# The down weight pieces of the experts are split into high and low parts whole instead of by halves

## The reference

```python
logits = h @ router                                   # (256, 8)
top_v, top_i = lax.top_k(logits, 2)
wts = jax.nn.softmax(top_v, axis=-1)
comb = jnp.sum(one_hot(top_i, 8) * wts[..., None], axis=-2)
return sum(comb[..., e:e + 1] * swiglu(h, w1[e], w3[e], w2[e]) for e in range(8))
# swiglu(h, w1, w3, w2) = (silu(h @ w1) * (h @ w3)) @ w2
# w1, w3: (1024, 3584) of each expert; w2, the down weights: (3584, 1024)
```

## Time and profile before

| what | value |
|---|---|
| runs | median 2206.45 us of 3 (2204.03 to 2206.86) |
| profiled execution | 2205.63 us |
| its span, first to last instruction | 2203.8 us |
| mean granted TensorE clock | 0.982 of full speed |
| PE matmul busy | 2104.9 us (96%) |
| DVE busy | 1772.6 us (80%) |
| ACT busy | 1176.0 us (53%) |
| experts, about 1187 to 2197 us: PE busy from 1240 to 2040 | 800.0 of 800 us |
| the same, DVE | 709.4 of 800 us |
| the same, ACT | 585.6 of 800 us |
| the same, DMA engines busy | 0.92 to 0.94, 347 to 368 GB/s |

### The profile page before, as it was taken

How to read it: one execution, slowest core, us unless ns; L and a number is a source line. 1 busy time by engine, 2 the same in 40 slices (tenths; PEclk the granted TensorE clock), 3 DMA queues, 4 the chain that set the end, 5 groups by cost and what they waited for, 6 DMA issues and landing times.

```text
span 2203.8 us, 28714 instructions
## 1 busy us (share of the span) xinstructions
PE 2104.9 (96%) x10154; PEld 1737.3 (79%) x10154; DVE 1772.6 (80%) x2268; ACT 1176.0 (53%) x1388; POOL 42.5 (2%) x84
## 2 busy tenths in 40 slices
PE   8988999997999998879997999999999999999997
PEld 6765888876888886758996888888888888888886
DVE  7777877877677676877866988888898988989895
ACT  3316333324333332534555777777677777777674
POOL 0000000000000000000000000000000000000000
PEclk9999999998999999999997999999999999999999
DMA  8500233453444443403464999989898999989893
GB/s 320 192 33 1 96 110 134 172 200 115 171 152 153 171 153 114 163 25 120 163 236 157 388 356 349 373 323 368 335 371 334 366 349 342 370 336 371 331 364 123
DMA packets 77289, 512.44 MB, mean 233 GB/s; under 512 B 8738, under 2 KB 9890, under 8 KB 22820
## 3 DMA queue, kind: packets, MB, share of 16 engines
q1 hardware_dynamic: 65700, 469.59, 56.7%
q0 software_dynamic: 11520, 41.95, 5.3%
HBM read 510.46 MB, written 1.05 MB: 232 GB/s over the span
## 4 chain that ended last, share of the span: by engine, by line
PE 82%; DVE 11%; ACT 3%; issue 2%; DMA 2%; SPq 0%; DVEq 0%; ACTq 0%; POOL 0%; POOLq 0%
PE bank L844 9%; PE bank L842 9%; PE bank L843 9%; PE bank L863 5%; PE bank L865 5%; PE bank L864 5%; PE bank L596 4%; PE bank L598 4%; PE bank L597 4%; PE bank L761 2%; PE bank L762 2%; PE bank L763 2%; PE bank L737 2%; PE bank L747 2%; PE bank L748 2%
## 5 line engine op out<-in xcount | busy, mean ns | idle before, releaser
L971 ACT ACTIVATE down_high<-W 128x1024 fp32r<-128x1024 f32 x224 | 237.1, 1064 | 139.3 <-PE bank L865 139.1
L1341 DVE TENSOR_TENSOR up_b_low<-W,up_b_high 128x2048 fp32r<-128x2048 f32 x112 | 256.6, 2291 | 56.5 <-ACT up_b_high L964 56.5
L1348 DVE TENSOR_TENSOR down_low<-W,down_high 128x1024 fp32r<-128x1024 f32 x224 | 271.8, 1223 | 31.6 <-ACT down_high L971 21.7
L1335 DVE TENSOR_TENSOR up_a_low<-W,up_a_high 128x2048 fp32r<-128x2048 f32 x112 | 255.9, 2284 | 1.9 <-ACT up_a_high L958 1.9
L596 PE MATMUL bank<-h_high,tile_high 128*128 128x512 f32 (+1 forms) x704 | 240.1, 341 | 13.0 <-DVE tile_low L1392 13.0
L597 PE MATMUL bank<-h_low,tile_high 128*128 128x512 f32 (+1 forms) x704 | 237.9, 338 | 0.0
L598 PE MATMUL bank<-h_high,tile_low 128*128 128x512 f32 (+1 forms) x704 | 237.7, 338 | 0.0
L958 ACT ACTIVATE up_a_high<-W 128x2048 fp32r<-128x2048 f32 x112 | 212.9, 1901 | 2.1 <-PE bank L844 2.1
L964 ACT ACTIVATE up_b_high<-W 128x2048 fp32r<-128x2048 f32 x112 | 213.1, 1903 | 0.0
L863 PE MATMUL bank<-down_high,mact_high 128*128 128x512 f32 x448 | 186.5, 416 | 2.6 <-DVE down_low L1348 2.6
L865 PE MATMUL bank<-down_low,mact_high 128*128 128x512 f32 x448 | 176.3, 394 | 0.0
(11 more groups left out here) (257 smaller groups left out, 4306.9 us busy)
## 6 DMA issues: line engine op xcount, KB each, us to landing
W<-in_moe_up SPq DMA_DIRECT2D x224, 1024.0 KB, 5.8
W<-in_moe_down SPq DMA_DIRECT2D x112, 1024.0 KB, 5.1
W<-in_w_mod_later POOLq DMA_DIRECT2D x80, 512.0 KB, 3.8
W<-in_ffn SPq DMA_DIRECT2D x33, 1024.0 KB, 4.8
W<-in_attn_blocks SPq DMA_DIRECT2D x24, 1280.0 KB, 6.0
W<-in_attn_blocks SPq DMA_DIRECT2D x22, 1024.0 KB, 5.9
W<-in_attn_blocks SPq DMA_DIRECT2D x8, 1536.0 KB, 6.7
shift_tiles<-in_w_mod_first SPq DMA_DIRECT2D x8, 512.0 KB, 14.4
```

The source lines that it names most:

```text
L1335: tt(al[u][:], raw_a[u].rearrange("p (k n) -> p k n", k=KD // 2), ah[u][:].bitcast(F32), ALU.subtract) \
L1341: tt(bl[u][:], raw_b[u].rearrange("p (k n) -> p k n", k=KD // 2), bh[u][:].bitcast(F32), ALU.subtract) \
L1348: tt(cl[:, h, :], raw_c[u][:, h * D:(h + 1) * D], ch[:, h, :].bitcast(F32), ALU.subtract) \
```

## The change

The two halves of a down piece are split by one instruction on ACT and one on DVE. `down_high` waits until both halves of the `down` before are used, `down(g)` waits once, ahead of its first matmul, for the whole low tile, and SP's wait counts pieces instead of halves. The matmuls, the tiles, their buffers, the order in each queue and the DMA sizes stay.

```diff
             def down_piece(n, g, u):
-                sp.wait_ge(S("down_low"), 2 * g + (2 * n * ALL_PAIRS - 2))
+                sp.wait_ge(S("down_low"), g + (n * ALL_PAIRS - 1))
                 sp.dma_start(raw_c[u], moe_down_in[g]).then_inc(S(f"raw_c_in{u}"), 16)
...
                 def down(g, u, start=False, stop=False):
                     pe.wait_ge(S("moe_act_low"), g + 1)
+                    pe.wait_ge(S("down_low"), g + 1)
                     for h in range(2):
-                        pe.wait_ge(S("down_low"), 2 * g + (h + 1))
                         a = slice(h * P, (h + 1) * P)
...
             def down_high(g, u, turn):
                 act.wait_ge(S(f"raw_c_in{u}"), turn * 16 + 16)
-                for h in range(2):
-                    act.wait_ge(S("down_used"), 2 * g + (h + 1))
-                    fn(ch[:, h, :], raw_c[u][:, h * D:(h + 1) * D], ACT.Copy).then_inc(S("down_high"), 1)
+                act.wait_ge(S("down_used"), 2 * g + 2)
+                fn(ch[:, :, :], raw_c[u].rearrange("p (h d) -> p h d", h=2), ACT.Copy).then_inc(S("down_high"), 1)
...
             def down_low(g, u):
-                for h in range(2):
-                    dve.wait_ge(S("down_high"), 2 * g + (h + 1))
-                    tt(cl[:, h, :], raw_c[u][:, h * D:(h + 1) * D], ch[:, h, :].bitcast(F32), ALU.subtract) \
-                        .then_inc(S("down_low"), 1)
+                dve.wait_ge(S("down_high"), g + 1)
+                tt(cl[:, :, :], raw_c[u].rearrange("p (h d) -> p h d", h=2), ch[:, :, :].bitcast(F32), ALU.subtract) \
+                    .then_inc(S("down_low"), 1)
```

## The result

The changed kernel took 2217.92 us, the median of 5 runs (2215.61 to 2219.14), against 2206.45 for the kernel before (2204.03 to 2206.86, 5 runs): ratio 1.0057, 95% interval 1.0045 to 1.0068. It is slower, by 11.5 us of the medians. The profiled execution took 2219.14 us, its span is 2217.3 us, 13.5 more than before.

A forecast was written before the change was run, and what follows sets the result against it. PE was taken as the bound, never idle from 1240 to 2040 us. Start 2.1, end 6.4 and clock 3.8 summed to +12.3 us on the profiled 2205.63, forecast 2218 us, range 2212.5 to 2220.5.

The forecast's parts named there:

- The steady turn: Expert turns under `up`: the whole split is still done in time, cost 0, with the turn staying 8.4 us.
- the 1.0 us to spare: Steady turn: low reaches PE at 1507.24, PE comes to the next `down` at 1508.27.
- The wait taken from PE: PE's `down` steps: one wait a turn fewer, taken as 0; slower steps allowed at most 4.0 us in 112 turns.
- The start: First turns of expert 0: PE waits for the later low tile before `down(0)` and `down(2)`, +2.1 us, bounds 1.1 and 2.2.
- The way through `keep_weighted`: Expert 0: later transposes delay ACT's `keep_weighted`, then `down_low(2)` behind it, so `down(2)` starts at 1226.45 instead of 1224.38.
- The end: Behind the last `up`: PE waits longer before `down(110)` and `down(111)`, +3.2 us, then +6.4 for both.
- The clock: Last two downs: PE's clock falls in gaps of 4.2 and 4.4 us, +3.8 us, bounds 0 and 5.0.
- The rival that it stays up: Last two gaps: clock stays up in one or both, 2216.0 us with one low, 2214.1 with none; chance 0.24.
- my bound of 5.0: Last two downs: upper bound of the clock's cost, 2.5 us each at half speed throughout.
- The sum: Whole kernel: 2.1 + 6.4 + 3.8 = +12.3 us on 2205.63, stated as 2218 us, 0.5% slower.
- Faster, by the rule of fewer instructions: Rival for all turns: the per-instruction saving reaches the end time, 18 to 25 us won, 2181 to 2188; chance 0.02.

The follow-up runs named there:

- E8: Changed kernel with an extra 2048-column ACT copy ahead of each `down_high` from expert 1 on; 2282.88 us, ratio 1.0356 to the kernel before.
- E5: Changed kernel, but only ACT copies whole pieces and DVE subtracts by halves; 2215.24 us, ratio 1.0045 to the kernel before.
- E6: Changed kernel, but ACT copies by halves and only DVE subtracts whole pieces; 2216.38 us, ratio 1.0046 to the kernel before.
- E4: Changed kernel with 16 unneeded matmuls in each of the two gaps behind the last `up`; 2214.23 us, ratio 1.0040 to the kernel before.
- E2: Changed kernel with the 14 pieces of expert 0 by halves again, all others whole; 2217.19 us, ratio 1.0058 to the kernel before.
- E7: Changed kernel with an extra 512-column ACT copy ahead of each `down_high` from expert 1 on; 2219.54 us, ratio 1.0068 to the kernel before.
- E3: Changed kernel with halves in expert 0 and the last two pieces, whole in the 96 between; 2205.18 us, ratio 0.9998 to the kernel before.
- E11: Halves in expert 0, whole pieces from expert 1 on, last two in tiles of their own; 2202.59 us, ratio 0.9988 to the kernel before.
- E10: Kernel before, by halves, with the last two down pieces split into tiles of their own; 2202.13 us, ratio 0.9985 to the kernel before.

## Why the prediction was right

- **The steady turn, 0.** Right: 946.41 us in both kernels. The copy came to 1.92 us and the subtraction to 2.29; E8 confirms the 1.0 us to spare, and the refill of the raw pieces stayed in time.
- **The wait taken from PE, 0.** Right: with the same middle, none of the 4.0 us that the slower steps would have allowed came back.
- **The start, +2.1.** It measured 2.16, with waits of 1.03 and 1.63 us where 1.0 and 1.5 were given. The way through `keep_weighted` is in the rows: ACT's idle time before it grew from 2.37 us to 3.53. E5 and E6 show that it is the subtraction by whole pieces that costs it: with ACT alone whole the start is 45.42 us, with DVE alone whole 47.61.
- **The end, +6.4.** 6.58 by E4 against the kernel before.
- **The clock, +3.8.** 3.56 in the changed kernel's profile. The rival that it stays up fell: the clock went down in, or in E6 once right behind, both gaps of all six profiles that had them unfilled (changed, E2, E5 to E8), with gaps of 3.21 to 6.28 us. But the size is less certain than the forecast made it look. What is left of the end over that of the kernel before, once the longer gaps are taken off, is 3.6 us in the changed kernel, 5.0 in E2 with the same instructions at the end, 3.9 in E5, 4.0 in E6, 4.9 in E7 and 4.0 in E8. It does not follow the length of the gaps, and what decides it is not shown. My 3.8 was taken from a single gap in layer 0; that this kernel's profile came so near is partly luck, and E2 and E7 lie at my bound of 5.0.
- **The sum.** 12.3 forecast, 12.3 by parts in the profiles, 11.5 between the medians. The time, 2217.92, was forecast as 2218; that it came so near is partly luck too, since runs of one kernel spread by 3 to 5 us.
- **Faster, by the rule of fewer instructions.** The saving is there, 22 and 15 us of busy time (the working had 25 and 18, from instructions 0.01 to 0.02 us shorter than these), but none of it reached the end time: ACT and DVE idle longer instead, and E3 is no faster than the kernel before, nor E11 than E10. The rule of the Trainium skill ("VectorE: DVE Perf Modes", section on the TRN2 errata) holds for the engines; it says nothing of who waits for them.

## What to carry to other kernels

Joining two halves of a pipelined step saves a fixed cost on engines that may have time to spare, and takes the overlap out of the chain through a single buffer. Here ACT copied one half under the `down` before and PE started on one half of low, so that PE had to wait 1.2 us between the last two downs; whole, all of the copy and all of the subtraction stand between them, 4.48 us. E5 and E6 show that joining the halves on one engine alone already costs most of it, gaps of 3.43 and 3.63 us. Compare the longer chain with the slack of the steady turn, and then look at the first and last turns, where the work that hides it is missing: here two pieces of 112 cost 10 us. In the drain, buffers of other stages lie free and can stand in for the missing second one: that took away the whole loss at the end, and the kernel before's own waits there too.

## What was unexpected in the hardware

- PE's clock fell in a gap of 3.21 us (E5), and it fell even after PE had come back from one of 3.42 us (E6).
- The length of the gap does not decide it alone. Far ahead of the experts, in code that is the same in both kernels, PE idles 2.03 us before 166.97 us in the profile before and 2.03 us before 166.93 in the changed one. Behind it the clock was down in the first (PEclk 0.60 over 4 us) and full in the second:

```profile
167.00:171.00 4.00, 4.00 (x16) 2.26 (x16) 3.79 (x13) 2.55 (x6) 0.00 (x0) 0.60 0.00 0
167.00:171.00 4.00, 3.54 (x20) 1.79 (x20) 3.79 (x13) 2.59 (x6) 0.00 (x0) 1.00 0.00 0
```

- With gaps of the same length, 4.26 and 4.48 us in the changed kernel and 4.35 and 4.57 in E2, seven matmuls of the first `down` and ten of the second, of twelve each, ran wholly at the low clock in the one, all twelve in both downs in the other.
- Sixteen matmuls that nobody needs, put into each gap, made the kernel 3.6 us shorter at the end.
